# Third mixer's entry in a two-block transformer kernel: the value projection first, tile 0's token products between the turns of tile 0 and tile 1

## The chip, the cores and the metric

The kernel runs on one core of one Trainium2 chip, in one launch. The metric is the device time of an execution in microseconds (us). A core has TensorE (PE, matmuls; its weight loads are PEld), VectorE (DVE), ScalarE (ACT), GpSimd (POOL) and SyncE (SP), which issues the weight loads from main memory. Each engine runs its own instructions in the order written and waits on semaphores that the others count up.

## The reference, cut to what matters

Two blocks stand one behind the other. The first is two layers of attention, Fourier mixing and a convolutional feed-forward part. The second is two mixers with a layer norm behind each. The change is in the last mixer, `_mixer_c`, which the kernel's author counts as the third; x has 256 tokens of 1024 features, all values are float32.

```python
def _mixer_c(h, w_in, lower_bounds, layer_idx, norm_gain, w_out):
    proj = jnp.einsum('bsd,df->bsf', h, w_in).astype(jnp.float32)
    q, f_f, f_b, i, gate = _split(proj, (C_WIDTH,) * 5)      # C_WIDTH = 12 heads * 128
    lb = jax.nn.softmax(lower_bounds.astype(jnp.float32), axis=0)
    lb = (jnp.cumsum(lb, axis=0) - lb[0])[layer_idx]
    heads = lambda t: t.reshape(Bsz, S, C_HEADS, C_HEAD_DIM)
    def forget(z):
        f = lb + (1.0 - lb) * jax.nn.sigmoid(z)
        return heads(1.0 - f), heads(jnp.log(f))
    k_f, g_f = forget(f_f)
    k_b, g_b = forget(f_b)
    qh = heads(jax.nn.silu(q)) * (C_HEAD_DIM ** -0.5)
    o = bidirectional_gated_scan(qh, k_f, g_f, k_b, g_b, heads(i))
    y = _head_rmsnorm(o, norm_gain) * jax.nn.silu(gate)
    return jnp.einsum('bsf,fd->bsd', y.astype(h.dtype), w_out)

# in second_block, after each mixer:
x = _layer_norm(DEEPNORM_ALPHA * x + y, ln_gain[layer], ln_bias[layer])
```

The scan turns the running sums of the log gates g into exponentials, scales q and k with them, takes scores within and between chunks of 32 tokens, masks them and multiplies them with the values i.

## The kernel before, in words

**Precision.** A product is made of three matmuls with rounded operands: coarse x coarse, coarse x fine, fine x coarse (`three`, L477 to L482). So each operand is split in a coarse part (a cast by ScalarE) and a fine part (what is left, by VectorE). The weights pass through `raw_w`, a ring of 2 slots; a chunk is 256 columns (`CHUNK8` = 8 x 256 elements in each of 128 partitions). `split` (L1131, the cast on L1137) and `fine` (L1830, L1838) fill one of two pairs of split weights. A slot is loaded again (L2895) when `fine` has read it, a pair is written again when the products of the chunk two ahead of it are done.

**The second layer's input.** The mixer before ends in `out_tail`: TensorE's last output products, then VectorE's layer norm for tile 0 (tokens 0 to 127) and tile 1, in `x_tok`. In this tail ScalarE casts the first chunk of the third mixer, and GpSimd makes its fine part. `turn_x` is in three engines' streams: TensorE transposes each tile in two halves of four blocks into a bank (L474), ScalarE takes the coarse part of a half out of the bank (L1152), VectorE the fine part (L1845), which also frees the bank. TensorE's `turn_x` ends in `evacuated()`, which waits until all banks have been read.

**The order of the entry.** The order is written out by hand, in each engine's stream for itself, and that of SyncE (`order`, at the end of its stream) must agree. Before: forget gates of the two directions (`C_K`, chunks 1 and 2), q (3), the values `C_V` (4), the output gate (5), the next group's forget gates (6, 7). `features()` multiplies a chunk into features x tokens: two units of 8 x 3 matmuls with 256 tokens each. `tokens()` multiplies into tokens x features, one unit for each tile: `token_product(xT, t, ...)` needs only tile t of x. The head groups (6 groups of 2 heads) follow in a loop, in which the projections of later groups fill in between the scans.

**The gate work.** VectorE's `forget(g)` (L2649, L2652) turns the sigmoids of chunks 1 and 2 into gates; ScalarE's `log_gates(g)` takes their Ln (L1720); VectorE's `c_decays` (from L2413) sums them and `exponentials` (L1596 to L1602) and `c_factors` (L2436 to L2454) make the scan's operands. TensorE's `scan_scores` (L914 to L935) multiplies them, VectorE masks the scores (L2468). In VectorE's stream `chunk()` is one `fine` and the skipping of two units, and it stands between these steps.

The code that the change touches, and what calls it:

Of the kernel before, what the change touches and what calls it, by code (L numbers as in the profile page):

```python
# [15 lines left out]
KD = D // P  # L16
# [36 lines left out]
C_GROUPS = C_HEADS // GROUP  # L53
# [11 lines left out]
COLS = 256  # L65
CHUNK8 = KD * COLS
# [20 lines left out]
X_UPDATES = 24  # L87
# [114 lines left out]
def two_block_kernel(nc, a, out):  # L202
    ctx = ExitStack()
    with ctx:
# [53 lines left out]
        def parts(name, at, *shape):  # L258

            return (rounded(name + "_coarse", at, *shape), rounded(name + "_fine", at + int(np.prod(shape)), *shape))  # L260
# [61 lines left out]
        xT = parts("x_turned", ACTS, KD, SEQ)  # L322
# [86 lines left out]
        def _(pe):  # L409
# [16 lines left out]
            def split_weights(k, n, loads=1):  # L426

                ring.next(loads)
                p = fine.n % PAIRS
                pe.wait_ge(fine_ready, fine.next())  # L430
                slot_release.append(("fine", fine.n))
                return [w[:, p, 0:k * n].rearrange("p (k n) -> p k n", k=k) for w in (w_co, w_fi)]
# [12 lines left out]
            def evacuated(reads=None):  # L445

                for b in range(GEMM_BANKS):
                    if u.reads[b]:
                        pe.wait_ge(bank_read[b], u.reads_now(b) if reads is None else reads[b])
# [19 lines left out]
            def transposes(ins, parts_in=P, width=P):  # L469

                ps = begin()
                for j, blk in enumerate(ins):
                    w = blk.shape[1]
                    mm = nc.tensor.transpose(ps[0:w, j * width:j * width + parts_in], blk, ident[0:parts_in, 0:parts_in])  # L474
                end(mm)
# [8 lines left out]
            def feature_product(w, k_rows, c0, acts, n):  # L484

                ps = begin()
                for k in range(k_rows):
                    mm = three(ps[:, 0:n], [v[:, k, c0:c0 + P] for v in w], [v[:, k, 0:n] for v in acts],
                               k == 0, k == k_rows - 1)
                end(mm)  # L490
# [8 lines left out]
            def token_product(acts, t, w, n):  # L499
                ps = begin()  # L500
                end(token_rows(ps[:, 0:n], acts, 0, t, w, KD, n, True, True))
# [383 lines left out]
                ffn_down(l)  # L885


            def turn_x(updates_of):
                for t in range(2):
                    for half in range(2):  # L890
                        pe.wait_ge(x_done, updates_of(t, half))
                        transposes([x_tok[:, t, k * P:(k + 1) * P] for k in range(4 * half, 4 * half + 4)])
                evacuated()

            def features():
                w = split_weights(KD, COLS)
                for j in range(2):
                    feature_product(w, KD, j * P, xT, SEQ)

            def tokens():  # L900
                w = split_weights(KD, COLS)
                for t in range(2):
                    token_product(xT, t, w, COLS)
# [139 lines left out]
            seen_next(y_ready)  # L1043
            out_last(rest)

            turn_x(lambda t, half: X_UPDATES + 2 * t + half + 1)
            for _ in range(3):
                features()
            tokens()
            for _ in range(3):  # L1050
                features()
            for g in range(C_GROUPS):
                v = c_in[g % 2][:, C_V, :].rearrange("p (t n) -> p t n", t=2)
# [27 lines left out]
        def _(act):  # L1081
# [14 lines left out]
            def take():  # L1096

                b = u.bank()
                act.wait_ge(gemm_done, u.event())
                return b, pb[b]  # L1100
# [9 lines left out]
            def step(ins):  # L1110

                ins.then_inc(act_done, 1)
                done.next()
# [13 lines left out]
            def copy_out(dst, m=P, n=512):  # L1127
                b, ps = take()
                read(nc.scalar.copy(dst, ps[0:m, 0:n]), b)

            def split(size, loads=1, ahead=0):  # L1131

                s, v = ring.next(loads)
                act.wait_ge(landed[s], v)
                act.wait_ge(gemm_done, u.made_now() + ahead)
                p = coarse.n % PAIRS
                nc.scalar.copy(w_co[:, p, 0:size], raw_w[:, s, 0:size]).then_inc(coarse_ready, 1)  # L1137
                coarse.next()
# [9 lines left out]
            def coarse_of(dst):  # L1148

                b, ps = take()  # L1150
                n = dst.shape[1] * dst.shape[2]
                nc.scalar.copy(dst, ps[:, 0:n].rearrange("p (k t) -> p k t", k=dst.shape[1])).then_inc(act_coarse, 1)  # L1152
# [403 lines left out]
                seen[y_ready].next(KD)  # L1556


            def turn_x():
                for t in range(2):  # L1560
                    for half in range(2):
                        coarse_of(xT[0][:, 4 * half:4 * half + 4, t * P:(t + 1) * P])

            def features_out(func, dst, scale=1.0):
                for j in range(2):
                    b, ps = take()
                    read(nc.scalar.activation(dst(j), ps[:, 0:SEQ], func, scale=scale), b)

            def features(func, dst, scale=1.0, following=CHUNK8):

                split(following)
                features_out(func, dst, scale)

            def tokens_out(dst):
                for t in range(2):
                    copy_out(dst[:, t, :], n=COLS)
# [132 lines left out]
            out_tail(CHUNK8)  # L1709

            step(nc.scalar.activation(small[:, 94:95], eps[:, 0:1], ACT.Sigmoid))
            turn_x()

            def input_half(g, which):
                return lambda j: c_in[g % 2][:, which, j * SEQ:(j + 1) * SEQ]

# [7 lines left out]

            def values(g):
                return c_in[g % 2][:, C_V, :].rearrange("p (t n) -> p t n", t=2)
            for d in range(2):
                features(ACT.Sigmoid, input_half(0, C_K + d))
            features(ACT.Silu, input_half(0, C_Q))
            split(CHUNK8)  # L1730
            log_gates(0)
            tokens_out(values(0))
            split(CHUNK8)
            exponentials(0, 1.0)
            split(CHUNK8, ahead=2)
# [38 lines left out]
        def _(dve):  # L1774
# [19 lines left out]
            def read(ins, b):  # L1794
                ins.then_inc(bank_read[b], 1)
# [45 lines left out]
            def fine_of(acts, k0, k, t0, t):  # L1841

                b, ps = take()
                seen_next(act_coarse)
                read(nc.vector.tensor_tensor(acts[1][:, k0:k0 + k, t0:t0 + t],  # L1845
                                             ps[:, 0:k * t].rearrange("p (k t) -> p k t", k=k),
                                             acts[0][:, k0:k0 + k, t0:t0 + t].bitcast(F32), ALU.subtract), b)
# [545 lines left out]
            assert n_x[0] == X_UPDATES  # L2393


            def turn_x():
                for t in range(2):
                    for half in range(2):
                        fine_of(xT, 4 * half, 4, t * P, P)

            def chunk(following=CHUNK8, units=2):

                fine(following)
                skip(units)
# [77 lines left out]
            def scan_norm(V, f0, gain0, gates, bufs=norm_bufs[0]):  # L2482

                osb, _, rsd = bufs
                nv = V // P
                units = GROUP * nv
                rb = rsd.rearrange("p (h t) -> p h t", h=GROUP)
                ov = osb[:, 0:units * SEQ].rearrange("p (h v t) -> p h v t", h=GROUP, v=nv)
                for vh in range(nv):
                    step(nc.vector.tensor_tensor(ov[:, :, vh, :], ov[:, :, vh, :], rb, ALU.mult))  # L2490
                settle()
                for un in range(units):
                    o = osb[:, un * SEQ:(un + 1) * SEQ]
                    step(nc.vector.scalar_tensor_tensor(out=o, in0=o, scalar=cols[:, 4, gain0 + un:gain0 + un + 1],
                                                        in1=gates[:, un, :], op0=ALU.mult, op1=ALU.mult))
                settle()
                split_here([v[:, f0:f0 + units, :] for v in y2T],
                           osb[:, 0:units * SEQ].rearrange("p (f t) -> p f t", f=units)).then_inc(y_ready, 1)
# [138 lines left out]
            out_tail(0, lambda: ab_norm(1), rest, CHUNK8)  # L2637


            turn_x()  # L2640

            def forget(g):

# [15 lines left out]
                factors(d, 4 + 2 * g + d, c_in[g % 2][:, C_Q, :], c_in[g % 2][:, C_K + d, :])  # L2659
            def c_norm(g):  # L2660
                scan_norm(C_DIM, 2 * g, T_HGRN + 2 * g, sgT[:, 2 * (g % 2):2 * (g % 2) + 2, :])
            for _ in range(2):
                chunk()
            forget(0)
            for _ in range(2):
                chunk()
            c_decays(0, 0)
            chunk()
            c_decays(0, 1)
# [209 lines left out]
        def _(sp):  # L2879
            n = [0]  # L2880
# [87 lines left out]
            out_weights(kview(a["w_out_ab_2"][0]))  # L2968
            w_c = kview(a["w_in_c_2"][0])
            early, late = (1, 2), (0, 3, 4)  # L2970
            order = [(part, 0) for part in early]
            for g in range(C_GROUPS):
                order += [(part, g) for part in late] + [(part, g + 1) for part in early if g + 1 < C_GROUPS]
            for part, g in order:
                at = part * C_WIDTH + g * COLS
                load([w_c[:, :, at:at + COLS]])
# [74 lines left out]
```

## Time and profile before

| what | us |
|---|---|
| median of 3 runs | 2003.89 |
| lowest and highest | 2001.19, 2007.61 |
| profiled execution, its own time | 2005.95 |
| its span in the profile | 2004.1 |
| TensorE busy in the span | 1885.0 (94%) |
| VectorE busy | 1163.5 (58%) |
| ScalarE busy | 933.8 (47%) |
| third mixer, from its first transposes to the end | 1726.28 to 2004.1 |

The profile is of one execution. Its times count from the start of the span. A busy share is an average over stages with different limits, so the rows below are from the stage of the change.

### The profile page before, as it was taken

Reading aid. Unit: us, or ns where it says so; the run is one execution under the profiler, and the core shown is the slowest. Engines: PE = TensorE matmul, PEld = TensorE weight load, DVE = VectorE, ACT = ScalarE, POOL = GpSimd, SP = SyncE. Lnnn points to the kernel's source line nnn. Section 1 sums busy time; section 2 is a strip of 40 time slices with the busy share of each in tenths; the row PEclk is TensorE's granted clock in tenths of the full one; section 3 lists DMA queues with packets and bytes.
Section 4 is the critical chain, followed back from the end, with each engine's and each line's share of the span. In section 5 each row is a group of like instructions: output and inputs, shape, how many; then the busy total and the mean of one; then the engine's idle time right before and its main releaser. Section 6 shows DMA issues by size and latency. Waiting matters only on the chain.

```text
span 2004.1 us, 31227 instructions
## 1 busy us (share of the span) xinstructions
PE 1885.0 (94%) x12063; PEld 1577.9 (79%) x12063; DVE 1163.5 (58%) x1802; ACT 933.8 (47%) x1427; POOL 197.0 (10%) x201
## 2 busy tenths in 40 slices
PE   5999999999998999999998889989998999899997
PEld 2875565788887888888774579989988888799996
DVE  3426566433446555523535555677744578789987
ACT  3327555333224333311437555455533656387682
POOL 4010001000011222210110000023301000100000
PEclk9999999999998999999998999989998999999999
DMA  9225678333332233232250037545556442544442
GB/s 303 96 78 168 195 226 264 96 94 94 89 105 85 87 102 98 90 115 95 93 160 6 1 96 188 183 133 182 192 177 222 127 127 86 167 148 147 139 138 104
DMA packets 262823, 265.36 MB, mean 132 GB/s; under 512 B 6310, under 2 KB 230928, under 8 KB 262720
## 3 DMA queue, kind: packets, MB, share of 16 engines
q1 hardware_dynamic: 257856, 249.32, 40.0%
q0 software_dynamic: 4416, 13.49, 2.1%
q8 instruction: 71, 1.16, 0.3%
q10 hardware_dynamic: 448, 1.12, 0.2%
q14 instruction: 32, 0.26, 0.0%
HBM read 262.81 MB, written 1.10 MB: 132 GB/s over the span
## 4 chain that ended last, share of the span: by engine, by line
PE 76%; DVE 12%; ACT 5%; DMA 3%; issue 2%; SPq 0%; DVEq 0%; ACTq 0%
PE bank L480 21%; PE bank L481 21%; PE bank L482 21%; PE bank L693 4%; DMA region<-in_w_mod 2%; DVE weights_fine L1838 2%; PE bank L710 2%; PE bank L474 2%; PE bank L538 2%; PE bank L527 2%; ACT weights_coarse L1137 2%; PE bank L700 1%; DVE region L2480 1%; DMA region<-in_w_in_ab 1%; DVE small L2163 1%
## 5 line engine op out<-in xcount | busy, mean ns | idle before, releaser
L1838 DVE TENSOR_TENSOR weights_fine<-region,weights_coarse 128x2048 fp32r<-128x2048 f32 (+2 forms) x181 | 417.8, 2308 | 366.2 <-ACT weights_coarse L1137 365.3
L1137 ACT CAST weights_coarse<-region 128x2048 fp32r<-128x2048 f32 (+3 forms) x185 | 354.9, 1918 | 338.4 <-PE bank L482 323.8
L480 PE MATMUL bank<-normed_coarse,weights_coarse 128*128 128x256 f32 (+1 forms) x1104 | 372.0, 337 | 12.3 <-issue 5.0
L481 PE MATMUL bank<-normed_fine,weights_coarse 128*128 128x256 f32 (+1 forms) x1104 | 371.3, 336 | 0.0
L482 PE MATMUL bank<-normed_coarse,weights_fine 128*128 128x256 f32 (+1 forms) x1104 | 371.1, 336 | 0.0
L480 PEld LDWEIGHTS bank<-normed_coarse,weights_coarse 128*128 128x128 f32 x1104 | 212.4, 192 | 34.0 <-issue 13.3
L482 PEld LDWEIGHTS bank<-normed_coarse,weights_fine 128*128 128x128 f32 x1104 | 212.3, 192 | 20.9
L481 PEld LDWEIGHTS bank<-normed_fine,weights_coarse 128*128 128x128 f32 x1104 | 212.4, 192 | 20.7
L480 PE MATMUL bank<-x_turned_coarse,weights_coarse 128*128 128x256 f32 x616 | 177.8, 289 | 8.7 <-DVE weights_fine L1838 4.2
L481 PE MATMUL bank<-x_turned_fine,weights_coarse 128*128 128x256 f32 x616 | 175.5, 285 | 0.0
L482 PE MATMUL bank<-x_turned_coarse,weights_fine 128*128 128x256 f32 x616 | 175.4, 285 | 0.0
L1477 ACT ACTIVATE region<-bank,cols 128x512 f32<-128x512 f32 (+1 forms) x88 | 59.1, 672 | 216.9 <-PE bank L482 216.9
L480 PEld LDWEIGHTS bank<-x_turned_coarse,weights_coarse 128*128 128x128 f32 x616 | 119.3, 194 | 12.5 <-DVE weights_fine L1838 5.4
L2274 DVE SCALAR_TENSOR_TENSOR region<-bank,cols,region 128x510 f32<-128x510 f32 (+1 forms) x88 | 54.1, 615 | 114.1 <-ACT region L1477 113.1
L481 PEld LDWEIGHTS bank<-x_turned_fine,weights_coarse 128*128 128x128 f32 x616 | 119.5, 194 | 0.0
L482 PEld LDWEIGHTS bank<-x_turned_coarse,weights_fine 128*128 128x128 f32 x616 | 119.4, 194 | 0.0
L1402 ACT ACTIVATE region<-bank,small,q_scale 128x512 f32<-128x512 f32 (+1 forms) x96 | 67.9, 707 | 96.0 <-DVE small L2166 93.1
L693 PE MATMUL bank<-region 96*128 96x512 f32 (+4 forms) x224 | 105.9, 560 | 3.6 <-ACT region L1353 1.5
L480 PE MATMUL bank<-weights_coarse,ffn_mid_coarse 128*128 128x512 f32 x264 | 102.8, 389 | 0.9 <-DVE region L2240 0.9
L481 PE MATMUL bank<-weights_fine,ffn_mid_coarse 128*128 128x512 f32 x264 | 102.7, 389 | 0.0
L482 PE MATMUL bank<-weights_coarse,ffn_mid_fine 128*128 128x512 f32 x264 | 102.7, 389 | 0.0
L474 PE MATMUL bank<-ident,region 128*128 128x128 f32 (+3 forms) x449 | 70.5, 290 | 32.1 <-DMA ident<-in_c_ident 7.5
(295 smaller groups left out, 3586.1 us busy)
## 6 DMA issues: line engine op xcount, KB each, us to landing
region<-in_w_mod SPq DMA_DIRECT2D x48, 1024.0 KB, 5.3
region<-in_w_up SPq DMA_DIRECT2D x44, 1024.0 KB, 5.1
region<-in_w_in_c SPq DMA_DIRECT2D x30, 1024.0 KB, 5.1
region<-in_w_in_ab SPq DMA_DIRECT2D x20, 1024.0 KB, 5.4
region<-in_w_in SPq DMA_DIRECT2D x32, 512.0 KB, 4.7
region<-in_w_down SPq DMA_DIRECT2D x16, 1024.0 KB, 5.0
region<-in_w_in SPq DMA_DIRECT2D x14, 1024.0 KB, 5.1
region<-in_w_in SPq DMA_DIRECT2D x16, 384.0 KB, 3.5
```

The costliest lines, as they stand in the source:

```text
L474: mm = nc.tensor.transpose(ps[0:w, j * width:j * width + parts_in], blk, ident[0:parts_in, 0:parts_in])
L480: nc.tensor.matmul(o, sc, mc, start=first, stop=False)
L481: nc.tensor.matmul(o, sc, mf, start=False, stop=False)
L482: return nc.tensor.matmul(o, sf, mc, start=False, stop=last)
L527: mm = nc.tensor.matmul(ps[:, 0:n], acts[:, k, t * P:(t + 1) * P], w[:, k, c0:c0 + n], start=(k == 0), stop=(k == k_rows - 1))
L538: mm = nc.tensor.matmul(ps[strip:strip + 2, 0:COLS], sil_c[:, k, :], w[:, k, :], start=(k < MOD_STRIPS), stop=(k >= KD - MOD_STRIPS))
L693: nc.tensor.matmul(pb[4 + J % 2][:, 0:keys_of(i)[1] * P], q, k, start=True, stop=True).then_inc(scores_done, 1)
L1137: nc.scalar.copy(w_co[:, p, 0:size], raw_w[:, s, 0:size]).then_inc(coarse_ready, 1)
L1402: nc.scalar.activation(p_sb[:, J % 2, 0:nk], src, ACT.Exp, bias=small[:, at + J % 4:at + 1 + J % 4], scale=q_scale[:, i // 16, i % 16:i % ...
L1477: nc.scalar.activation(acc[:, j, 0:n], ps[:, 0:n], ACT.Identity, scale=cols[:, 2 * l, bass.ds(c + T_TAP1, 1)], bias=cols[:, 2 * l + 1, bas ...
L1838: nc.vector.tensor_tensor(w_fi[:, p, 0:size], raw_w[:, s, 0:size], w_co[:, p, 0:size].bitcast(F32), ALU.subtract).then_inc(fine_ready, 1)
L2274: link(nc.vector.scalar_tensor_tensor(out=a_s[:, :, 1:SEQ], in0=u_s[:, :, 0:SEQ - 1], scalar=cols[:, 2 * l, bass.ds(f + T_TAP0, 1)], in1=a ...
```

## The change

The chunk of values moves from the fourth to the first place of the third mixer's weights, in all four streams. TensorE transposes tile 0, waits for its banks, multiplies tile 0's values, and then does the same for tile 1; all forget gates and q follow. ScalarE copies tile 0's values out between its coarse parts of the two tiles, splits the next chunk, and copies tile 1's values; its `log_gates(0)` now follows q's output where it stood between the split of chunk 5 and the output of the values. VectorE skips one unit between the tiles, and its `forget(0)` stands one `chunk()` later. The `turn_x` of the second mixer keeps its order (no `behind`).

```diff
@@ TensorE
-            def turn_x(updates_of):
+            def turn_x(updates_of, behind=None):
                 for t in range(2):
                     for half in range(2):
                         pe.wait_ge(x_done, updates_of(t, half))
                         transposes([x_tok[:, t, k * P:(k + 1) * P] for k in range(4 * half, 4 * half + 4)])
-                evacuated()
+                    if t or behind:
+                        evacuated()
+                    if behind:
+                        behind(t)
...
-            turn_x(lambda t, half: X_UPDATES + 2 * t + half + 1)
-            for _ in range(3):
-                features()
-            tokens()
-            for _ in range(3):
+            first = []
+
+            def first_tokens(t):
+                if t == 0:
+                    first.extend(split_weights(KD, COLS))
+                token_product(xT, t, first, COLS)
+            turn_x(lambda t, half: X_UPDATES + 2 * t + half + 1, first_tokens)
+            for _ in range(6):
                 features()
@@ ScalarE
-            def turn_x():
+            def turn_x(behind=None):
                 for t in range(2):
                     for half in range(2):
                         coarse_of(xT[0][:, 4 * half:4 * half + 4, t * P:(t + 1) * P])
+                    if behind:
+                        behind(t)
...
-            turn_x()
-
...
+            def first_tokens(t):
+                if t:
+                    split(CHUNK8)
+                copy_out(values(0)[:, t, :], n=COLS)
+            turn_x(first_tokens)
             for d in range(2):
                 features(ACT.Sigmoid, input_half(0, C_K + d))
             features(ACT.Silu, input_half(0, C_Q))
-            split(CHUNK8)
             log_gates(0)
-            tokens_out(values(0))
             split(CHUNK8)
             exponentials(0, 1.0)
             split(CHUNK8, ahead=2)
@@ VectorE
-            def turn_x():
+            def turn_x(behind=0):
                 for t in range(2):
                     for half in range(2):
                         fine_of(xT, 4 * half, 4, t * P, P)
+                    if t == 0:
+                        skip(behind)
...
-            turn_x()
+            turn_x(1)
...
+            chunk(units=1)
             for _ in range(2):
                 chunk()
             forget(0)
-            for _ in range(2):
-                chunk()
+            chunk()
             c_decays(0, 0)
             chunk()
             c_decays(0, 1)
@@ SyncE
-            order = [(part, 0) for part in early]
+            order = [(3, 0)] + [(part, 0) for part in early]
             for g in range(C_GROUPS):
-                order += [(part, g) for part in late] + [(part, g + 1) for part in early if g + 1 < C_GROUPS]
+                order += [(part, g) for part in late if part != 3 or g] + [(part, g + 1) for part in early if g + 1 < C_GROUPS]
```

## Rows read from the trace of the kernel before

**Rows 1.** The page: busy us of each engine (share), and the chain's shares.

```profile
PE 1885.0 (94%) x12063; PEld 1577.9 (79%) x12063; DVE 1163.5 (58%) x1802; ACT 933.8 (47%) x1427; POOL 197.0 (10%) x201
...
PE 76%; DVE 12%; ACT 5%; DMA 3%; issue 2%; SPq 0%; DVEq 0%; ACTq 0%
```

**Rows 2.** The chain of waits, third mixer's entry: start us, us, what.

```profile
1728.59 3.17 DVE x_tok L2544 x2
...
1732.68 1.98 PE bank L474 x8
...
1735.37 0.70 DVE x_turned_fine L1845
1736.16 0.55 PE bank L480
...
1761.01 1.91 ACT weights_coarse L1137
...
1782.63 0.73 DVE region L2468
...
1783.50 0.36 PE bank L480
```

**Rows 3.** The timeline of TensorE: start, length, line, out<-in, count, idle before.

```profile
1726.28 1.03 PE L474 MATMUL bank<-ident,x_tok 128*128 128x128 f32 x8
1732.68 1.97 PE L474 MATMUL bank<-ident,x_tok 128*128 128x128 f32 x8 [5.36 <-DVE x_tok L2550]
...
1736.52 0.41 PE L481 MATMUL bank<-x_turned_fine,weights_coarse 128*128 128x256 f32 x1
...
1738.65 0.41 PE L482 MATMUL bank<-x_turned_coarse,weights_fine 128*128 128x256 f32 x1
...
1741.10 0.28 PE L480 MATMUL bank<-x_turned_coarse,weights_coarse 128*128 128x256 f32 x1
...
1743.14 0.28 PE L482 MATMUL bank<-x_turned_coarse,weights_fine 128*128 128x256 f32 x1
```

**Rows 4.** Stretches, TensorE: length, busy (instructions), granted clock, DMA share, GB/s.

```profile
1727.00:1732.00 5.00, 0.32 (x3) 1.00 0.00 0
1732.00:1732.50 0.50, 0.00 (x0) 0.74 0.29 51
...
1739.00:1739.50 0.50, 0.50 (x6) 0.93 0.42 164
...
1743.00:1778.00 35.00, 35.00 (x294) 1.00 0.50 161
```

**Rows 5.** The timeline of VectorE.

```profile
1733.20 2.01 DVE L1845 TENSOR_TENSOR x_turned_fine<-bank,x_turned_coarse 128x512 fp32r<-128x512 f32 x3
...
1759.39 1.22 DVE L2413 TENSOR_TENSOR_SCAN region<-region 128x512 f32<-128x512 f32 x1
...
1762.95 2.29 DVE L1838 TENSOR_TENSOR weights_fine<-region,weights_coarse 128x2048 fp32r<-128x2048 f32 x1 [0.50 <-ACT weights_coarse L1137]
1765.15 1.22 DVE L2415 TENSOR_TENSOR_SCAN region<-region 128x512 f32<-128x512 f32 x1
...
1768.50 2.29 DVE L1838 TENSOR_TENSOR weights_fine<-region,weights_coarse 128x2048 fp32r<-128x2048 f32 x1 [0.29 <-ACT weights_coarse L1137]
```

**Rows 6.** The timeline of ScalarE.

```profile
1735.17 1.91 ACT L1137 CAST weights_coarse<-region 128x2048 fp32r<-128x2048 f32 x1
...
1757.17 1.28 ACT L1720 ACT_TABLE_LOAD   x1
1758.46 1.16 ACT L1720 ACTIVATE region<-region 128x512 f32<-128x512 f32 x2
...
1760.74 0.37 ACT L1129 COPY region<-bank 128x256 f32<-128x256 f32 x1 [0.87 <-PE bank L482]
```

**Rows 7.** SyncE's queue: chunk 4's load is issued; all twelve loads, us to landing.

```profile
1739.50 0.37 SPq L2895 DMA_DIRECT2D region<-in_w_in_c  x1
...
region<-in_w_in_c SPq DMA_DIRECT2D x12, 1024.0 KB, 5.1
```

## The prediction

> **What bounds the kernel now.** I read the page first. Its busy shares and its chain of waits [rows 1] say that TensorE works for 94% of the span and carries 76% of the chain, so a change pays only where TensorE stands still, or where it is made to. Then I read the chain in order of time around the third mixer's entry [rows 2], and the timelines of TensorE, VectorE and ScalarE there [rows 3, 5, 6].
>
> The reader is to see a hole and a full stretch. The hole: TensorE turns tile 0 of x from 1726.28 to 1727.31, waits for VectorE's layer norm of tile 1, turns that from 1732.68 to 1734.65, and waits again for the splitting of the turned tile until 1736.16 [rows 2, 3]. Its granted clock falls from full (2.4 GHz) to half (1.2 GHz) in the hole, at about 1732.25, and comes back at about 1739.06 [rows 4]. The full stretch: from 1743 to 1778 TensorE has work in every microsecond [rows 4]. The chain leaves TensorE at 1761.01 all the same and runs over ScalarE and VectorE to the masked copy of the first scan's scores at 1782.63, which lets TensorE go on at 1783.50 after 0.5 us of idling [rows 2]. So in that stretch two things are nearly tied: seven chunks of products, and the gate work that follows the first two of them. A change that delays either moves the end.
>
> I number the chunks of 256 weight columns by their place in the stream. Before: forget gates 1 and 2, q 3, values 4, output gate 5, next group's gates 6 and 7, its q 8. After: values 1, forget gates 2 and 3, q 4, and 5 to 8 as they were. No instruction is added or dropped except a second round of waits on bank reads, whose cost is the wait itself; what changes is order.
>
> **Part 1, the entry.** The first product of tile 0 needs both its fine halves. VectorE makes them behind the layer norm of tile 1, in the change as before: three fine halves run from 1733.20 for 2.01 us, so the second ends at 1734.54 [rows 5]. The product can start at about 1734.65 where products started at 1736.16: 1.5 us gained. It does not reach into the 5.4 us of the hole itself.
>
> It starts at the half clock, at 0.213 us from matmul to matmul (2.13 us for the ten steps from 1736.52 to 1738.65) against 0.12 at full clock (2.04 us for 17 steps from 1741.10 to 1743.14) [rows 3]. If the clock comes back at the same 1739.06, the 24 matmuls take 20.7 slow steps and 3.3 fast ones and end at 1739.46. Before, 13 were slow; 7.7 more at 0.093 cost 0.7 us.
>
> TensorE's queue is in order, so the transposes of tile 1, which had run at 1732.68 under VectorE's work, now stand behind this product. They take 1.03 us at full clock (the first tile's row) [rows 3], to 1740.5. Behind them come ScalarE's coarse halves and VectorE's fine halves: before, 1.5 us passed from the last transpose (1734.65) to the first product (1736.16); here the transposes are shorter, so that the two fine halves queue up a little, and I take 1.6. The product of tile 1 starts at 1742.1, a gap of 2.65 us between the two. It takes 24 times 0.12, to 1745.0.
>
> Chunk 2's coarse part stands on ScalarE behind tile 1's coarse halves, at 1741.2 instead of 1735.17; 1.91 us of it [rows 6] and 2.29 us of fine part [rows 5] give 1745.4, so TensorE waits 0.4 us more. The entry's sum is -1.5 + 0.7 + 2.65 + 0.4 = +2.2 us.
>
> Chunk 4's load is issued when the fine part of chunk 2 is done, and that moves from 1739.50 to 1745.4; with 5.1 us to land [rows 7] it is there at 1750.5. ScalarE wants it after chunk 2's products, about 1751.9. That is hidden, with 1.4 us to spare. The other loads keep more.
>
> The clock has bounds. If it rose as long after the first product as before (2.9 us, at 1737.55), 7 matmuls fewer would be slow and the entry cost 1.6. If it did not rise until after the product of tile 1, all 48 matmuls and the 8 transposes (1.97 us instead of 1.03) would be slow: 0.3 + 0.9 + 2.2 = 3.4 more, less the 0.4 wait that this hides, entry +5.2. I take the middle, since the same clock change is the nearest row. The page "TensorE: Matmul & The Clock Gate" of the Trainium skill (Part 4) says that transposes do not count as TensorE work for the clock. By that rule the 2.65 us between the products would be a pause, which could put off the rise, towards the +5.2. The trace shows the clock still full after 5 us of pause, so I leave the middle.
>
> **Part 2, the gate chain.** Before, ScalarE took the logarithms of the gates (table load at 1757.17, then two Ln of 1.16 us together) while TensorE worked on the values, chunk 4, whose last bank it read only at 1760.74 [rows 6]. After, chunk 4 is q, its reading comes first in ScalarE's order, and the logarithms stand behind its end. Chunk 4 ends 2.2 us later: last read at 1762.9, done 1763.3, table load 1.28 to 1764.6, first Ln done at about 1765.2.
>
> Only then can VectorE start the first decays, which began at 1759.39 [rows 5]. Behind them in its order is the fine part of chunk 6. Before, decays began at 1759.39 and that fine part at 1762.95 (ready for it 3.05 us after the decays began); it was done at 1765.2, and TensorE reached chunk 6 at 1743.26 + 4 x 5.76 = 1766.3 (a chunk is 48 x 0.12 = 5.76 us). After: 1765.2 + 3.05 + 2.3 = 1770.6 against TensorE's 1766.3 + 2.2 = 1768.5. TensorE waits about 2.1 us, and the shift grows to 4.3. Here the cover is gone that hid the logarithms.
>
> Then VectorE has the second decays (from 1765.15 to 1768.2 before) and the fine part of chunk 7, ready at 1775.9; TensorE reaches chunk 7 at 1776.4, no wait. The factors of both directions, chunk 8's fine part and the next group's forget gates follow in VectorE's order. Before, 14.1 us passed from the fine part of chunk 7 (1768.50) to the masked copy (1782.63). Now that fine part starts at 1773.6, so the copy starts at 1787.7 and chunk 8 at 1788.6: the shift is 5.1 us, all of it against 1783.50.
>
> From there the order is that of before, each group of the loop hangs on the one ahead of it, and nothing gives the time back: +5.1 us. The profiled execution took 2005.95 us (its span is 2004.1, 1.85 lie around it) and would come to 2011.05. That execution was 2.06 above the median of the three runs, so for the median I say 2003.89 + 5.1 = 2009.0.
>
> A rule that speaks for more: "ScalarE: Activation LUTs" of the Trainium skill (What ACT_TABLE_LOAD costs) gives 1.28 us for a table load and 1.38 us of drain besides. With that drain on the path the sum would be 6.5 and the time 2010.4. The trace has the 1.28 and no drain: load at 1757.17, Ln at 1758.46 [rows 6], so I leave it out.
>
> **Rivals.**
> - *Entry alone* (25%). TensorE's stream is the bound and the late logarithms hide. For it: TensorE was full until 1778 [rows 4] and waited 0.5 us after. Against it: the fine part of chunk 6 had only 1.1 us to spare and is now over 3 us later against TensorE. Time: 2003.89 + 2.2 = 2006.1.
> - *Clock stays low through both products of the values* (15%). The price of the bound above, entry +5.2; the gate chain adds 2.9 as before: 2003.89 + 8.1 = 2012.0. For it: the longer pause; against it: the row in which 2.9 us of products were enough.
> - *Faster* (4%). The product of tile 0 runs under the layer norm of tile 1: up to 24 x 0.12 = 2.9 us of work leaves the full stretch, 2003.89 - 2.9 = 2001.0. It decides only if both fine halves of tile 0 are ready before about 1729.8, so that 2.9 us fit ahead of 1732.68. VectorE's order puts them behind the norm, at 1734.54. The milder form, the start 1.5 earlier and a gap below 0.4 us between the products, is excluded by the transposes alone (1.03).
> - *No effect* (4%): start and gap cancel and the logarithms hide, 2003.9.
>
> **How the numbers follow.** The forecast (+5.1, 52%) has its own range of 3.9 to 6.6: the early clock takes 0.6 off, and each link of the chain is uncertain by some tenths. A difference of 0.3% is 6.0 us, about what a measurement of this kernel can tell from no change. Three runs spread from 2001.19 to 2007.61, so a median is itself good to about 1.5 us. Over 2009.9 are most of the clock case (0.12) and nearly half of the forecast with that spread (0.22): slower 0.35. Faster by 6 us has no mechanism of that size: 0.03. The rest, 0.62, is within. For the range I go down to 2004.3, which takes in the entry alone and leaves out most of no effect and faster, and up to 2013.0, which holds the clock case.
>
> **What the profile after would show.** TensorE's first x_turned product near 1734.65 into the entry, 24 of them, then eight transposes, then a gap of some 2.6 us in all; TensorE waiting about 2 us for a weights_fine just before chunk 6; the first Ln behind, not ahead of, the last read of chunk 4; the first decays about 5.8 us later than before; the masked copy near 1787.7. If chunk 6 does not wait, part 2 is wrong. If the first product starts by 1731, part 1 is. What would make the prediction wrong beyond that: a clock that never falls in the hole, or a weight load that comes late for chunk 4.

## The result, and the profile after

Over 20 runs each, the median rose from 2003.95 to 2009.78 us (before 1999.25 to 2007.74, after 2005.94 to 2017.36). The ratio is 1.0031, with a 95% interval of 1.0020 to 1.0042: 4.0 to 8.4 us slower, around the 6.0 us (0.3%) that the prediction took for what a measurement of this kernel can tell. The forecast was 2009.0.

The profiled execution took 2008.82 us, with a span of 2007.0. It reached the entry 2.9 us earlier than that of before, in code that the change does not touch (tile 1's norm passes start at 1725.67 instead of 1728.59 [rows 2]). So I compare lengths, not clock times: from VectorE's aggregate, the instruction that closes tile 1's norm statistics (1728.35 before, 1725.43 after), to the first matmul of chunk 8 (1783.50 [rows 2], 1786.53 after). That is 55.15 us before and 61.10 after: 5.95 us longer. From chunk 8 to the end of the span it is 220.6 and 220.5, so the whole loss lies in this stretch. To bring a time of the trace after into the frame of before, add 2.92. The aggregate in VectorE's timeline, kernel before:

```profile
1728.35 0.21 DVE L2539 BATCH_NORM_AGGREGATE small<-small 128x2 f32<-128x12 f32 x1
```

The page after, the busy line and the chain's shares:

```profile
PE 1884.9 (94%) x12063; PEld 1577.7 (79%) x12063; DVE 1163.4 (58%) x1802; ACT 933.6 (47%) x1427; POOL 197.0 (10%) x201
...
PE 76%; DVE 13%; ACT 5%; DMA 3%; issue 2%; SPq 1%; DVEq 0%; ACTq 0%
```

Against [rows 1] no engine works longer. In the chain VectorE's share rises from 12% to 13% and that of SyncE's queue (SPq) from 0% to 1%. Averages show no more than that; the chain in order of time, kernel after (start us, us, what; line numbers have moved by up to 11):

```profile
1725.43 0.22 DVE small L2550
1725.67 3.17 DVE x_tok L2555 x2
...
1730.36 1.21 DVE x_turned_fine L1854 x2
1731.57 0.38 issue
1731.95 0.55 PE bank L480
...
1737.41 0.72 PE bank L474 x4
1738.15 0.59 ACT x_turned_coarse L1158
1738.84 0.70 DVE x_turned_fine L1854
1739.54 0.80 issue
1740.34 0.36 PE bank L480
...
1761.45 1.28 ACT L1726
1762.74 0.64 ACT region L1726
1763.41 1.24 DVE region L2424
...
1766.47 2.20 DVE weights_fine L1847
...
1771.63 2.20 DVE weights_fine L1847
...
1785.66 0.73 DVE region L2479
...
1786.53 0.36 PE bank L480
```

Against [rows 2] the reader is to see two things. The chain comes to TensorE twice in the entry, before and after. Before, its first visit was the eight transposes of tile 1 alone (1732.68, 1.98 us), and all products followed the second. Now the first visit is tile 0's 24 products and then the transposes (1731.95 to 1738.13 on the chain), and the way over ScalarE and VectorE back to TensorE comes once more behind them. And the chain leaves TensorE behind chunk 4 for ScalarE's table load and Ln (L1726), which did not stand on it in this stretch before, and then follows VectorE's decays straight into the fine parts of chunks 6 and 7.

TensorE's timeline after, the rows that answer to [rows 3]:

```profile
1723.36 1.03 PE L474 MATMUL bank<-ident,x_tok 128*128 128x128 f32 x8
...
1731.95 0.55 PE L480 MATMUL bank<-weights_coarse,x_turned_coarse 128*128 128x256 f32 x1 [7.55 <-DVE x_turned_fine L1854]
...
1737.21 1.34 PE L474 MATMUL bank<-ident,x_tok 128*128 128x128 f32 x8
1740.34 0.36 PE L480 MATMUL bank<-weights_coarse,x_turned_coarse 128*128 128x256 f32 x1 [1.79 <-DVE x_turned_fine L1854]
...
1768.72 0.39 PE L480 MATMUL bank<-x_turned_coarse,weights_coarse 128*128 128x256 f32 x1 [1.96 <-DVE weights_fine L1847]
...
1786.53 0.36 PE L480 MATMUL bank<-x_turned_coarse,weights_coarse 128*128 128x256 f32 x1 [0.99 <-DVE region L2479]
```

The 24 matmuls between 1731.95 and 1737.21 are tile 0's values, all of them slow. The wait of 1.96 us stands in front of chunk 6, in a stretch that had no pause [rows 4]. ScalarE after, answering to [rows 6]: the last read of q's bank and then the logarithms.

```profile
1761.05 0.38 ACT L1575 ACTIVATE region<-bank 128x256 f32<-128x256 f32 x1 [1.88 <-PE bank L482]
1761.45 1.28 ACT L1726 ACT_TABLE_LOAD   x1
1762.74 1.15 ACT L1726 ACTIVATE region<-region 128x512 f32<-128x512 f32 x2
```

TensorE's clock, kernel after (length, busy, granted clock, DMA share, GB/s): it fell at about 1727.6, 3.2 us behind the transposes of tile 0, where in [rows 4] it had been 4.9 us. It came back at about 1737.8, 10.2 us after its fall, where it had been 6.8 us.

```profile
1727.50:1728.00 0.50, 0.00 (x0) 0.59 0.00 0
...
1737.50:1738.00 0.50, 0.50 (x5) 0.67 0.00 0
```

### The profile page after: what moved, and what is told of

The parts are those of the page before. It is cut to its first block, busy times and chain, and to the rows that moved or that the text cites. A ratio compares the mean times of both kernels' runs of the same rounds, so it can differ in the third digit from the quotient of the medians.

```text
span 2007.0 us, 31229 instructions
## 1 busy us (share of the span) xinstructions
PE 1884.9 (94%) x12063; PEld 1577.7 (79%) x12063; DVE 1163.4 (58%) x1802; ACT 933.6 (47%) x1427; POOL 197.0 (10%) x201
## 4 chain that ended last, share of the span: by engine, by line
PE 76%; DVE 13%; ACT 5%; DMA 3%; issue 2%; SPq 1%; DVEq 0%; ACTq 0%
PE bank L480 21%; PE bank L481 21%; PE bank L482 21%; PE bank L693 4%; DVE weights_fine L1847 3%; PE bank L710 2%; DMA region<-in_w_mod 2%; PE bank L538 2%; PE bank L527 2%; PE bank L474 2%; PE bank L700 1%; ACT weights_coarse L1143 1%; DVE region L2491 1%; DMA region<-in_w_in_ab 1%; DVE small L2172 1%
## 5 line engine op out<-in xcount | busy, mean ns | idle before, releaser
L480 PE MATMUL bank<-weights_coarse,normed_coarse 128*128 128x512 f32 (+3 forms) x272 | 94.8, 349 | 4.8 <-DVE normed_fine L1985 3.9
```

Source lines behind the costliest of these rows:

```text
L480: nc.tensor.matmul(o, sc, mc, start=first, stop=False)
```

## The experiments

In all of them "length" is that from tile 1's aggregate to chunk 8's first matmul, unless the expectation counts from the norm passes (0.24 us less). Each length is of the one profiled execution. "Slow steps" are steps of 0.19 us or more from one matmul to the next among the first products; up to 3 of them are no clock's. The 16 slow steps that e3 and e9 each have in chunk 6 are not counted. "At full clock" takes 0.093 us off for each slow step, where the clock fell. It does not take off what slow transposes cost, so it is good to about half a microsecond: for the kernel before it gives 54.0, and e10, in which the clock did not fall, has 53.6. Each ratio is against the kernel before on the same chip, with 11 or 12 runs of the experiment (20 of the kernel after).

| kernel | length | slow steps | at full clock | wait ahead of chunk 6 | ratio (95%) |
|---|---|---|---|---|---|
| before | 55.15 | 12 | 54.0 | none | 1 |
| after | 61.10 | 24 | 58.9 | 1.96 | 1.0031 (1.0020 to 1.0042) |
| e1 logarithms early | 58.48 | 24 | 56.2 | none | 1.0006 (0.9993 to 1.0018) |
| e2 before, logarithms late | 59.16 | 26 | 56.7 | 1.94 | 1.0013 (1.0003 to 1.0023) |
| e3 both tiles turned first | 58.23 | 13 | 57.0 | 1.95 | 1.0013 (1.0001 to 1.0024) |
| e4 order of chunks alone | 56.92 | 27 | 54.4 | none | 1.0000 (0.9989 to 1.0010) |
| e5 after, 40 extra matmuls | 60.05 | 18 | 58.4 | 1.95 | 1.0014 (1.0001 to 1.0027) |
| e6 before, 40 extra matmuls | 54.99 | 13 | 53.8 | none | 0.9996 (0.9984 to 1.0007) |
| e7 fine parts early | 56.27 | 18 | 54.6 | 1.95 | 1.0014 (1.0003 to 1.0026) |
| e8 e7 and logarithms early | 55.11 | 30 | 52.3 | none | 1.0001 (0.9988 to 1.0013) |
| e9 after, filled | 58.78 | 2 | 58.8 | 1.95 | 1.0021 (1.0009 to 1.0032) |
| e10 before, filled | 53.57 | 0 | 53.6 | none | 0.9993 (0.9980 to 1.0007) |
| e11 e8, filled | 53.00 | 3 | 53.0 | none | 0.9992 (0.9980 to 1.0003) |

**e1: the logarithms back ahead of q's output.**

```diff
-            features(ACT.Silu, input_half(0, C_Q))
-            log_gates(0)
+            split(CHUNK8)
+            log_gates(0)
+            features_out(ACT.Silu, input_half(0, C_Q))
```

> The changed kernel with ScalarE's logarithms of the first gates put back ahead of the output of q. I compare lengths from VectorE's first norm pass over tile 1 to the first matmul of chunk 8: 54.9 us before (1783.50 - 1728.59), 60.9 after (1786.53 - 1725.67). Two-part theory (entry about 3.1, late logarithms about 2.8): no wait of TensorE ahead of chunk 6, decays about 3 us earlier against TensorE, length 58.7, time about 2 us under the changed kernel. Rival (the entry alone costs, the late logarithms hide): length stays 60.9.

Measured 58.23 from the norm passes, with the same 24 slow steps as after, and no wait ahead of chunk 6. The two parts stand, and the late logarithms are worth 2.6 us (61.10 to 58.48). The rival in which they hide falls. The whole-run ratio shows less: 1.0006 puts e1 only 1.2 us over before (-1.4 to 3.6), where its length is 3.3 over. The interval holds both.

**e2: the kernel before with late logarithms.**

```diff
             split(CHUNK8)
-            log_gates(0)
             tokens_out(values(0))
+            log_gates(0)
```

> The kernel before with one move only: ScalarE takes the logarithms of the first gates behind the output of chunk 4 (here the values). The entry is untouched. Two-part theory: decays start 3.7 us later, TensorE waits about 2.1 us for the fine part of chunk 6, length 57.7, time +2.8 us over before. Rival (late logarithms hide): length 54.9, no wait, time as before.

Measured 58.92 from the norm passes, 1.2 over the expectation. The wait of 1.94 us came where it was expected:

```profile
1767.12 0.39 PE L480 MATMUL bank<-x_turned_coarse,weights_coarse 128*128 128x256 f32 x1 [1.94 <-DVE weights_fine L1838]
```

The 1.2 us are the clock's: 26 slow steps in an entry whose code is that of before, where there were 12. This was the first sign that two executions of one code differ here by over a microsecond. At one clock the part costs 2.7 us, and the ratio (0.6 to 4.6 us) agrees.

**e3: the new order of chunks, but both tiles turned first.**

```diff
-            turn_x(lambda t, half: X_UPDATES + 2 * t + half + 1, first_tokens)
+            turn_x(lambda t, half: X_UPDATES + 2 * t + half + 1)
+            for t in range(2):
+                first_tokens(t)
```

(ScalarE and VectorE follow: both tiles' parts, then `split` and `tokens_out`.)

> The changed kernel's order of chunks and its late logarithms, but both tiles are turned before the first product, as before. Two-part theory: the entry's 3.1 us are gone, the gate part stays: length 57.7, wait of about 2 us ahead of chunk 6, time +2.8 over before. Rival (the split entry is what is paid and the rest hides): length 54.9. Second rival (bringing the values first costs by itself, since gates come a chunk later): length over 58.5.

Measured 57.99 from the norm passes, wait 1.95: as the two-part theory has it. The entry's part is gone and the gate part has stayed. (0.24 us of this length are a second fall of the clock, in chunk 6; see e9.)

**e4: only the order of the chunks.** The edits of e1 and e3 together.

> Values first, both tiles turned first, logarithms ahead of q's output: only the order of the chunks differs from before. Two-part theory: length 54.9 to 55.3, no wait ahead of chunk 6, time as before within 0.5 us. Rival (gates a chunk later are too late by themselves): length over 56.5, with VectorE's decays or factors late.

Measured 56.67 from the norm passes, 1.4 over the upper end, and just over the rival's 56.5. But there is no wait ahead of chunk 6, there are 27 slow steps where before had 12, and 15 of them at 0.093 are those 1.4 us. At full clock it is 54.4 against 54.0, and the ratio is 1.0000. Bringing the values first costs nothing by itself that these measurements can tell (the ratio reaches 2 us either way); the rival falls, by the ratio and the missing wait more than by the length.

**e5 and e6: extra work against the falling clock.** Both kernels do 40 matmuls more, whose result nobody reads:

```diff
+                        for _ in range(40):
+                            nc.tensor.matmul(pb[6][:, 0:COLS], y2T[0][:, 0, 0:P], y2T[0][:, 0, :], start=True, stop=True)
```

> The changed kernel with 40 more matmuls of 256 columns in the hole, behind tile 0's transposes, into a bank that nobody reads (about 4.8 us at full clock, done before the fine parts of tile 0). Theory of the clock's share: the granted clock no longer falls there, tile 0's 24 matmuls go at 0.12 instead of 0.213 us, transposes at 1.03: 2.2 + 0.3 = 2.5 us less, length from tile 1's norm to chunk 8 about 58.3 instead of 60.9, time 2 to 3 us under the changed kernel, and no runs above 2014 us if those are the clock's. Rival (the entry is paid by the order of the waits alone): length stays near 60.9 or only moves by tenths.

> The kernel before with the same 40 matmuls in its hole (5.4 us of waiting for tile 1). Theory: clock stays full, 12 slow steps and the slow transposes go: 1.1 + 0.9 = 2.0 us, length about 52.9 instead of 54.9, time 2 us under before, up to 3.3 where 26 steps are slow. Rival (the gate chain over VectorE and ScalarE holds the end here): length within 0.5 of 54.9.

Both missed. The clock still fell, later and for 3.4 us, now at the start of the products (18 and 13 slow steps). By its length e6 meets the condition of its rival (54.75 from the norm passes), but with the clock fallen it could not tell the two apart; e10 does. The pauses that were left were 2.8 us in e5, and 0.65 and 1.8 us in e6. Lengths fell by 1.05 and 0.16. So it takes less pause than I had thought, and e9 and e10 below leave none above 1 us.

**e7: what the change would need.** The coarse parts of tile 0 go ahead of ScalarE's root of tile 1, the fine parts ahead of VectorE's norm passes:

```diff
# cut to the moves; both out_tail functions, in the loop over t, ahead of the root (ScalarE), ahead of the norm passes (VectorE)
+                    if t and inside:
+                        inside()
...
# ScalarE
-            out_tail(CHUNK8)
+            out_tail(CHUNK8, lambda: [coarse_of(xT[0][:, 4 * half:4 * half + 4, 0:P]) for half in range(2)])
...
# VectorE
-            out_tail(0, lambda: ab_norm(1), rest, CHUNK8)
+            out_tail(0, lambda: ab_norm(1), rest, CHUNK8, lambda: [fine_of(xT, 4 * half, 4, 0, P) for half in range(2)])
```

(What is left of `turn_x` in both streams, tile 1's parts, is written out behind this.)

> The changed kernel, but tile 0's coarse parts stand ahead of ScalarE's root of tile 1 and its fine parts ahead of VectorE's two norm passes over tile 1. That is what the change would need to fill the hole. Length is counted from the last norm statistic of tile 1 (its aggregate) to chunk 8: 55.2 before, 61.1 in the changed kernel. Theory: tile 0's product starts when GpSimd's fine part of chunk 1 is done, about 2.9 us behind the aggregate instead of 6.5; transposes of tile 1 follow within 3 to 4 us; entry 3.2 us under before, late logarithms 2.9 over it: length 54.9, time as before. Rival (VectorE is what binds, and 1.3 us put ahead of the norm come out at the end): length over 60.

Tile 0's product started 2.8 us behind the aggregate, and what it waited for last was GpSimd's fine part of chunk 1 (timeline of TensorE, e7):

```profile
1729.51 0.36 PE L480 MATMUL bank<-weights_coarse,x_turned_coarse 128*128 128x256 f32 x1 [3.85 <-POOL weights_fine L2777]
```

The length was 56.3 instead of 54.9, with 18 slow steps where I had counted on none (1.7 us); the late logarithms were in it still, as expected, with their wait of 1.95 us. At full clock 54.6, 4.3 less than after. The mechanism was right, its size was the clock's again; the ratio says 0.6 to 5.2 us slower than before, so the forecast "time as before" missed.

**e8: e7 with e1's edit.**

> The kernel of early fine parts with ScalarE's logarithms ahead of q's output as well. Theory: length from the aggregate about 52.5, time 2 to 3 us under before. If the clock falls all the same, 54.5 and time as before. Rival: no better than early fine parts alone, since the masked copy of the first scan binds.

Length 55.1, with 30 slow steps: the clock fell twice, from 1728 and again from 1735. At full clock it is 52.3, near the 52.5 expected, and the best order so far; at the clock that it got, it runs as the kernel before does.

**e9, e10, e11: the same clock for all.** The pauses of after, before and e8 are filled with 60, 44 and 30 extra matmuls behind tile 0's transposes, and 12 behind tile 1's.

> The changed kernel with 60 extra matmuls behind tile 0's transposes and 12 behind tile 1's, so that TensorE has no pause above 1 us in the entry. Length from tile 1's aggregate to chunk 8, without its slow steps: 61.1 - 24 x 0.093 - 0.3 = 58.6. Theory: no low clock, length 58.6, with waits ahead of chunk 6 (2 us) and the gap of 3 us between the two products of the values still there. If the clock falls all the same, something other than TensorE's pauses makes it fall. Time about 2.5 us under the changed kernel.

> The kernel before, filled in the same manner: 44 matmuls in the hole, 12 behind tile 1's transposes. Theory: no low clock, length 55.15 - 12 x 0.093 - 0.9 = 53.1, time 2 to 3 us under before. The difference to the filled changed kernel is then the price of the change at one clock: 5.5 us by the theory (3 entry less 0.3, 2.8 logarithms). Rival (half or more of the change's cost is the clock's): difference under 3 us.

> Tile 0's fine parts early, logarithms ahead of q's output, 30 extra matmuls in the hole and 12 behind tile 1's transposes. The earlier run of it without the extra matmuls had length 55.1 with 32 slow steps, so 52.1 at full clock. Theory: length 52.1, time 2.5 to 4 us under before. Rival (extra matmuls delay what stands behind them): length over 53.5.

The clock stayed full through all three entries; none of the pauses left was above 0.84 us. Lengths 58.78, 53.57 and 53.00, against 58.6, 53.1 and 52.1. e9, VectorE's and TensorE's timelines:

```profile
1734.35 0.21 DVE L2553 BATCH_NORM_AGGREGATE small<-small 128x2 f32<-128x12 f32 x1
...
1792.02 1.60 DVE L2482 COPY_PREDICATED region<-tri,bank 128x512 f32<-128x512 uint32 x2
```

```profile
1775.08 0.39 PE L480 MATMUL bank<-x_turned_coarse,weights_coarse 128*128 128x256 f32 x1 [1.95 <-DVE weights_fine L1850]
...
1793.13 0.37 PE L480 MATMUL bank<-x_turned_coarse,weights_coarse 128*128 128x256 f32 x1
```

e10, the same:

```profile
1724.85 0.21 DVE L2541 BATCH_NORM_AGGREGATE small<-small 128x2 f32<-128x12 f32 x1
...
1777.55 1.60 DVE L2470 COPY_PREDICATED region<-tri,bank 128x512 f32<-128x512 uint32 x2
```

```profile
1778.42 0.36 PE L480 MATMUL bank<-x_turned_coarse,weights_coarse 128*128 128x256 f32 x1 [0.47 <-DVE region L2470]
```

The change costs 58.78 - 53.57 = 5.2 us with the clock full in the entry (5.5 expected), so the rival in which the clock makes half of it falls. A little of that is still the clock's: in e9 it fell once more, in chunk 6 (last section). TensorE came late to chunk 8 by that: e9's row has no wait there, and the matmul stands 1.11 us behind the start of the masked copy, where it is 0.87 after and in e10. Counted to the masked copy, the length is 57.67 in e9 and 52.70 in e10, and the change costs 5.0 us. So of the 5.95 us between the two profiles, 0.7 to 1.0 us were the clock's. The filled e11 is 0.6 us shorter than the filled before, less than the 1 us expected: GpSimd's fine part of chunk 1 took 5.69 us in e11 and 5.07 in e8, and tile 0's product starts behind it. Why it took longer is not shown. (The expectation of e11 counts 32 slow steps in e8, the table 30; with 30 it would have been 52.3.) The ratio of e11, 0.9992, has 1 in its interval. The 2 to 3 us that e10's expectation forecast are not shown in whole runs either: its ratio is 0.9993, also with 1 in the interval. No version was shown to beat the kernel before.

## Why the prediction was right

By its own steps, in the frame of before:

| step | forecast | measured |
|---|---|---|
| first product starts | -1.5 | -1.3 (1734.87) |
| more slow steps | +0.7 | +1.1 |
| gap between the two products | +2.65 | +3.13 (1737.21 to 1740.34) |
| chunk 2's weights late | +0.4 | +0.2 |
| entry, to chunk 2 | +2.2 | +3.1 (1743.47 + 2.92 against the prediction's 1743.26) |
| first decays start | 1765.2 | 1766.3 |
| wait ahead of chunk 6 | 2.1 | 1.96 |
| fine part of chunk 7 to masked copy | 14.1 | 14.1 (from 1771.55) |
| masked copy | +5.1 | +5.95 |

**The entry.** The mechanism was right: the product cannot start until VectorE is through tile 1's norm, and the transposes that ran under that norm come out into the open. Two terms were too small. The gap: I had 1.6 us from the last transpose to the next product, and it was 1.79 in after, e1, e5 and e7; the transposes took 1.34 us and not 1.03, since the first of them ran before the clock was back. And the clock: it came back 5.9 us after the first product began, not 4.4, so all 24 matmuls were slow, not 21. It had also fallen earlier, 3.2 us into the hole and not 4.9. My 21 lay between what the runs show: 24 slow steps in after and e1, 18 in e5 and e7, whose pauses were other ones. These two terms are the 0.9 us by which the entry, and with it the whole forecast of +5.1 against +5.95, came out short. The load of chunk 4, the other thing that could have gone wrong, was hidden as said: its cast started at 1749.81 with no wait for it.

**The gate chain.** It went link by link as worked out, from the logarithms over the decays to the fine part of chunk 6. e1 takes it away and e2 makes it alone: 2.6 us, and 2.7 at one clock, against 2.9 forecast. e4 shows that it is not the later gates themselves: with them a chunk later and the logarithms in their old cover nothing is lost. So it is one statement's place on ScalarE, behind the read of a bank whose products are still running.

**Table loads and transposes.** The page "ScalarE: Activation LUTs" of the Trainium skill (What ACT_TABLE_LOAD costs) gives 1.38 us of drain beside each table load. By the prediction's sum that would have been +6.5 us. The trace after shows Ln at 1762.74, 0.01 us behind the end of a load that began at 1761.45 and took 1.28, and the masked copy moved by 5.95. The measurement decides against the drain here. The page "TensorE: Matmul & The Clock Gate" of the Trainium skill (Part 4) says that a transpose does not count as TensorE's work for the clock in the way that a matmul does. No run here tells whether it holds: none has the same pauses with and without transposes in them.

**The rivals.** Entry alone (2006.1) is out by e1, e2 and the wait ahead of chunk 6. The clock case did not come as it was put: the clock was back at 1737.8, ahead of the second product at 1740.34. What the clock took of the change was 0.7 to 1.0 us between the two profiles, not the 3 us of that case. Faster (product under tile 1's norm) did not happen for the reason given, and e7 shows that it needs two moves in VectorE's and ScalarE's order and then has GpSimd's fine part as its next limit.

**Luck.** The forecast of 2009.0 stands on a median of three runs, 2003.89, whose spread was 6.4 us. That it came within 0.1 us of the median of 20, 2003.95, is luck, and so is part of the nearness of 2009.0 to 2009.78. The steps above are what the prediction can be measured by.

## What to carry to other kernels

Before moving work into a hole, ask which in-order queue feeds it: here TensorE was idle for 5.4 us, but the operand stood behind a layer norm on VectorE, and what moved ahead of tile 1's transposes only took away their cover. When streams written by hand are reordered, look at what each statement was hidden under, not only at what it needs: the logarithms had half a chunk of cover and lost it by one place. And compare short stretches of the trace between two fixed events, with the slow clock steps counted: they gave every part to half a microsecond, where 11 or 12 whole runs told 2 us apart at best.

## What I had not expected of the hardware

**The clock falls after shorter pauses than in [rows 4].** There TensorE stood for 4.9 us before its clock fell. It was 3.2 us in the kernel after and 2.7 in e1, with the same code up to there. In e6 the pauses were 0.65 and 1.78 us with eight transposes between them, and the clock fell at about 1732.1 all the same, 0.2 us before the products began. In e9 a wait of 1.95 us ahead of chunk 6 was followed by half clock within chunk 6, from 0.9 us behind its first matmul (1775.08), though TensorE worked on it without a pause (stretches of e9):

```profile
1774.00:1775.00 1.00, 0.00 (x0) 1.00 0.00 0
1775.00:1776.00 1.00, 0.92 (x7) 0.99 0.00 0
1776.00:1777.00 1.00, 1.00 (x7) 0.50 0.66 165
1777.00:1778.00 1.00, 1.00 (x7) 0.50 1.05 368
```

e3 had the same at 1764; after, e2, e5 and e7 had the same wait and kept their clock there. What decides between the two is not shown.

**VectorE's norm passes take longer beside GpSimd's work.** The hole that the change aimed at is in part two norm passes of VectorE over tile 1. The same two passes over tile 0 took 1.41 us (VectorE and GpSimd, kernel before):

```profile
1722.74 1.41 DVE L2544 SCALAR_TENSOR_TENSOR x_tok<-x_tok,small 128x512 f32<-128x512 f32 x2
...
1725.82 5.40 POOL L2757 TENSOR_TENSOR weights_fine<-region,weights_coarse 128x512 fp32r<-128x512 f32 x4 [203.14 <-ACT weights_coarse L1137]
```

Over tile 1 they took 3.17 us, from 1728.59 [rows 2], while GpSimd made the fine part of chunk 1 until 1731.2. In e7, where less of them fell into GpSimd's work, they took 2.46. No run moved that fine part elsewhere, so what it would give is open.

**One code, many times.** e9's profiled execution took 2015.68 us, where its median is 2009.36. Against the profile of before it was 6.2 us behind already at 400 us, in code that both share, and never got them back. The clock can account for most of that: over these 400 us the mean granted clock, taken over stretches of 20 us, was 0.966 in e9 and 0.979 before. By my estimate that is at most 400 x 0.013 = 5.2 us. It was not the clock of the third mixer's entry, which stayed full in e9. So the condition in e5's expectation, that executions above 2014 us are those of the clock in the entry, does not hold for this one, though e5 itself had none above 2010.90. The executions after the change that took 2016 to 2017 us (4 of 20) may be of the same kind: their mean granted clocks are 0.972 to 0.978, and 14 of the other 16 have 0.979 or more. None of the four was profiled, so where they lost it stays open. The spread between executions is as large as the change.
